# The second block's head outputs are turned in another order, and the branch products begin with the differential branch

## The reference, cut to what matters

```python
o_mla = mla_attention(q, k, v_mla).reshape(b, s, BRANCH_WIDTH)                        # latent heads
od = diff_attention(dq, dk, dv, positions, lam, slopes[WIN_HEADS:])
o_diff = (rms_norm(od, g_diff_out) * (1.0 - lam_init)).reshape(b, s, BRANCH_WIDTH)    # differential heads
o_win = window_attention(wq, wk, wv, positions, win_sink, slopes[:WIN_HEADS])         # banded heads
gates = jax.nn.sigmoid(gate_logits.reshape(b, s, N_BRANCH, D_MODEL))
merged = (gates[:, :, 0] * (o_mla @ w_branch[0])
          + gates[:, :, 1] * (o_diff @ w_branch[1])
          + gates[:, :, 2] * (o_win @ w_branch[2]))
x = x + merged @ w_out
```

## Time and profile before

| | |
|---|---|
| median of three runs | 1748.23 us (1746.33 to 1748.44) |
| the profiled execution, its own time | 1745.46 us |
| its span in the trace | 1743.6 us |
| TensorE busy with matmuls | 1670.2 us of the span |
| VectorE, ScalarE, GpSimd busy | 1172.7, 920.7, 443.6 us |
| mean granted TensorE clock, in parts of full speed | 0.987 |

### The profile page before, as it was taken

One profiled execution on the slowest core, in us unless ns is written; L12 is line 12 of the kernel. 1 busy time (PEld: TensorE's weight loads), 2 busy tenths in 40 slices (PEclk: granted clock), 3 DMA queues, 4 the chain that ended last, 5 costly groups with the idle time before them and its releaser, 6 DMA issues.

```text
span 1743.6 us, 30149 instructions
## 1 busy us (share of the span) xinstructions
PE 1670.2 (96%) x11354; PEld 1520.1 (87%) x11354; DVE 1172.7 (67%) x1609; ACT 920.7 (53%) x1576; POOL 443.6 (25%) x184
## 2 busy tenths in 40 slices
PE   8989999999989999999999999999899999999997
PEld 6878799988887899978899989999788999899996
DVE  5687754458786644476784777666758856777667
ACT  5654544446645544465655564444665555554445
POOL 2212222212222222224511122222235211222222
PEclk9989999999999999999999999999999999999999
DMA  8432455556423655546323455665464333566653
GB/s 329 154 122 91 150 201 181 190 160 208 155 77 115 229 181 182 182 144 227 125 97 111 134 190 183 209 196 177 150 214 156 106 101 115 172 205 199 203 179 126
DMA packets 82563, 288.74 MB, mean 166 GB/s; under 512 B 9051, under 2 KB 11908, under 8 KB 81924
## 3 DMA queue, kind: packets, MB, share of 16 engines
q1 hardware_dynamic: 77352, 272.58, 47.7%
q10 hardware_dynamic: 5084, 14.37, 2.4%
HBM read 284.81 MB, written 2.11 MB: 165 GB/s over the span
## 4 chain that ended last, share of the span: by engine, by line
PE 62%; DVE 7%; ACT 2%; issue 2%; DVEq 0%; ACTq 0%
PE bank L716 30%; PE bank L733 25%; DVE w_lo L682 2%; PE bank L1287 2%; PE bank L1268 1%; PE bank L1259 1%; PE bank L761 1%; PE bank L1247 1%; ACT w_hi L678 1%; PE bank L1300 0%; DVE qk L2513 0%; PE bank L906 0%; PE bank L1179 0%; PE bank L914 0%; DVE z L2105 0%
## 5 line engine op out<-in xcount | busy, mean ns | idle before, releaser
L682 POOL TENSOR_TENSOR w_lo<-raw,w_hi 128x1024 fp32r<-128x1024 f32 x146 | 376.6, 2579 | 1225.6 <-ACT w_hi L678 1225.6
L682 DVE TENSOR_TENSOR w_lo<-raw,w_hi 128x1024 fp32r<-128x1024 f32 x364 | 555.9, 1551 | 155.2 <-ACT w_hi L678 153.8
L678 ACT ACTIVATE w_hi<-raw 128x1024 fp32r<-128x1024 f32 x510 | 519.9, 1051 | 107.3 <-PE bank L716 47.4
L716 PE MATMUL bank<-x_t_hi,w_hi 128*128 128x256 f32 x1984 | 326.7, 287 | 5.5 <-ACT gl L1423 3.0
L716 PE MATMUL bank<-x_t_lo,w_hi 128*128 128x256 f32 x1984 | 319.8, 284 | 0.0
L716 PE MATMUL bank<-x_t_hi,w_lo 128*128 128x256 f32 x1984 | 319.5, 283 | 0.0
L716 PEld LDWEIGHTS bank<-x_t_hi,w_hi 128*128 128x128 f32 x1984 | 279.0, 192 | 18.0 <-issue 5.7
L716 PEld LDWEIGHTS bank<-x_t_lo,w_hi 128*128 128x128 f32 x1984 | 274.5, 192 | 0.0
L716 PEld LDWEIGHTS bank<-x_t_hi,w_lo 128*128 128x128 f32 x1984 | 274.3, 192 | 0.0
L733 PE MATMUL bank<-w_hi,x_t_hi 128*128 128x512 f32 (+3 forms) x448 | 134.5, 383 | 9.1 <-issue 5.8
L733 PE MATMUL bank<-w_hi,x_t_lo 128*128 128x512 f32 (+3 forms) x448 | 131.5, 376 | 1.5 <-DVE x_t_lo L1946 1.5
(11 more groups left out here) (391 smaller groups left out, 2134.5 us busy)
## 6 DMA issues: line engine op xcount, KB each, us to landing
raw<-stream SPq DMA_DIRECT2D x511, 512.0 KB, 4.3
rows<-rows ACTq DMA_DIRECT2D x4, 1024.0 KB, 4.7
gain<-rows ACTq DMA_DIRECT2D x8, 512.0 KB, 4.2
hv_p<-hv_dram ACTq DMA_DIRECT2D x14, 256.0 KB
x<-x_in SPq DMA_DIRECT2D x2, 512.0 KB, 4.9
bias_r<-rev_dram SPq DMA_DIRECT2D x1, 1024.0 KB, 7.3
hv_dram<-hv ACTq DMA_DIRECT2D x2, 512.0 KB, 6.9
y_out<-x SPq DMA_DIRECT2D x2, 512.0 KB, 2.7
```

What stands on the lines that cost most here:

```text
L678: self.eng.activation(w_hi[:, i, :], raw[:, i, :], ACT.Copy).then_inc(hi_done.sem, 1)
L682: self.eng.tensor_tensor(w_lo[:, i, :], raw[:, i, :], w_hi[:, i, :].bitcast(F32), ALU.subtract).then_inc((lo_pool if self.part == "pool" e ...
L716: mm = pe.matmul(target, a[:, i, w0 + kt * P:w0 + (kt + 1) * P], b[:, k0 + kt, :], start=kt + k == 0, stop=k == 2 and kt == kts - 1)
```

## The change

TensorE no longer waits for `o3_ready` ahead of the six pieces. It waits for the banded heads' part instead, turns the four differential and banded pieces, then waits for `o3_ready` and turns the two latent ones. ACT and DVE take the pieces in the same new order. Of the branch products the differential one of output tile 0 (`br1`) comes first, then the latent one (`br0`), then the banded one (`br2`) and the others as before. The bank table follows, so that pieces and products get banks in the new order. Amounts of work and numbers of instructions stay as they are.

```diff
+OT_ORDER = (2, 3, 4, 5, 0, 1)
...
-    work(*[f"ot{j}" for j in range(6)], *[f"br{i}" for i in range(24)])
+    work(*[f"ot{j}" for j in OT_ORDER], "br1", "br0", *[f"br{i}" for i in range(2, 24)])
...
-                pe.wait_ge(*c["o3_ready"](at, 1))
-                for j in range(6):
+                pe.wait_ge(*banks.read(at, "owin"))
+                for j in OT_ORDER:
+                    if j == 0:
+                        pe.wait_ge(*c["o3_ready"](at, 1))
                     transposed(at, f"ot{j}", lambda k, t: o3[:, t, (2 * j + k) * P:(2 * j + k + 1) * P])
 
-                for i in range(24):
+                for i in (1, 0, *range(2, 24)):
                     b = i % 3
                     pe.wait_ge(*banks.free(at, f"br{i}"))
                     if i < 3:
-                        pe.wait_ge(*x_hi(at, 8 + 2 * b))
+                        pe.wait_ge(*x_hi(at, 8 + OT_ORDER.index(2 * b)))
...
                     feature_major(at, uid[f"br{i // 2}"], bank[banks.bank(at, f"br{i}")][:, 0:S], o_t_hi, o_t_lo, 4,
-                                  begin=i % 2 == 0, w0=i % 2 * 512, k0=4 * b, split=split if i < 3 else None).then_inc(*banks.fills(at, f"br{i}"))
+                                  begin=i == 1 or i % 2 == 0 and i > 0, w0=i % 2 * 512, k0=4 * b, split=split if i < 3 else None).then_inc(*banks.fills(at, f"br{i}"))
...
-                for j in range(6):
+                for j in OT_ORDER:
                     if j in (2, 3):
                         round_gained(at, f"ot{j}", o_t_hi[:, 2 * j:2 * j + 2, :], lambda k: par2("g_do"))
...
-                for j in range(6):
+                for n, j in enumerate(OT_ORDER):
                     hi, lo = o_t_hi[:, 2 * j:2 * j + 2, :], o_t_lo[:, 2 * j:2 * j + 2, :]
                     if j in (2, 3):
-                        rest_gained(at, f"ot{j}", 7 + j, hi, lo, lambda k: par2("g_do"))
+                        rest_gained(at, f"ot{j}", 7 + n, hi, lo, lambda k: par2("g_do"))
                     else:
-                        rest_of_bank(at, f"ot{j}", 7 + j, hi, lo)
+                        rest_of_bank(at, f"ot{j}", 7 + n, hi, lo)
```

## The result

The changed kernel took 1750.2 us (median of 18 runs, 1747.91 to 1754.26), the kernel before in the same sessions 1746.53 us. The ratio is 1.0024, with a 95% interval of 1.0016 to 1.0031: 4.2 us slower, most likely. By the medians it is 3.7 us. The change touches two short places of an execution of 1750 us.

A forecast was written before the change was run, and what follows sets the result against it. TensorE, busy 1670.2 of 1743.6 us, was taken as the bound, with ScalarE's sigmoids on the chain before the products. Bank 0.9 + clock 2.2 = 3.1 us on the 1748.23 us median gave 1751.3 us, range 1747.5 to 1753.0.

The forecast's parts named there:

- The waiting engine: Before the branch products: ScalarE's table and sigmoids set the first rounding, so turning pieces during TensorE's 1.67 us wait gains nothing.
- The bank of the first product: Bank 7, held by the third piece, comes free later, so the first product starts 0.43 us later per layer, 0.9 in all.
- my sign of 6.3 to 6.4 us: Sign of being right: first product starts 6.3 to 6.4 us behind the last weighing in both layers, in place of 5.93.
- The latent pieces: Turned, rounded and rested last, they cost the latent product nothing, with 0.6 us of room before its last four matmuls.
- The clock: A 3.0 us TensorE idle stretch before the products drops its clock to half in both layers, costing 2.2 us in all.
- I take 1.1 us: Chosen loss per layer from half clock on the products, out of 0.9 to 1.5 us, for a stretch of 3.4 us.
- the forecast: Main case, chance 0.50: first product 0.43 us later per layer and half clock in both layers; 1750.9 to 1751.7 us.
- slower than can be missed: Rival, chance 0.20: half clock lies wholly on the products in both layers, 3.9 us in all, 1752.1 us or more.
- within 0.2%: Outcome that the whole kernel's time stays within 0.2% (about 3.5 us) of before, given 0.68.
- a real gain: Rival, chance 0.04: without sigmoids ahead of the roundings, 1.67 us come off each layer, 3.3 us in all, 1744.9 us.
- no change: Rival, chance 0.03: the first product is not later and TensorE keeps full speed, 1748.2 us.
- a clock that holds: Rival, chance 0.23: TensorE's speed doesn't fall at the products, or falls in one layer alone; 1749.1 to 1750.2 us.

The follow-up runs named there:

- e2: Changed kernel with the wait for the latent heads put back ahead of the first piece, all orders staying changed; ratio 1.0003 to the kernel before.
- e3: Changed kernel with ScalarE's table load and first two sigmoids moved behind the six roundings; ratio 0.9987 to the kernel before.
- e1: Changed kernel with TensorE's idle stretch filled by 24 useless transposes per layer, ahead of turning the last banded piece; ratio 1.0008 to the kernel before.
- e8: Kernel before with only the two banded pieces moved to idle banks 0 and 1, orders and sigmoids as before; ratio 0.9991.
- e5: e3 with, in addition, the two banded pieces moved to idle banks 0 and 1; ratio 0.9985 to the kernel before.
- e7: Changed kernel run again unaltered for a second profile; ratio 1.0019 to the kernel before.
- e9: e5 with, in addition, ScalarE and VectorE taking the pieces in the order differential, latent, banded; 1739.61 us against 1747.62, ratio 0.9957.
- e4: Kernel before with only ScalarE's table load and two sigmoids moved behind the six roundings, old orders kept; ratio 0.9994.
- e10: e5 run once more unaltered, on another chip; ratio 0.9985 to the kernel before.

## Why the prediction was right, and what was off

**The waiting engine.** Right. The chain said that ScalarE's table and sigmoids set the first rounding and that the early pieces are worth nothing. The first rounding stayed at 3.2 us, e2 shows the same start with and without early pieces, and e3 shows that the pieces become worth something as soon as ScalarE is free.

**The bank of the first product.** Right in mechanism and size: 0.43 us per layer expected, 0.39 measured in e1 and in the second layer of e2. That the bank decides is shown by e8, and by e5 against e3. In the changed kernel itself a second thing stands behind it. At the half clock TensorE's own last eight transposes take 1.94 us, and the first product, which comes behind them in the queue, starts at 6.64 us in place of 6.34 (6.51 in one layer of e7). My sum had the product wait for VectorE alone, so my sign of 6.3 to 6.4 us came in one of the four layers.

**The latent pieces.** Costed at nothing, by 0.6 us of room. Right for the changed kernel: its products have no wait. The room was the reason that it stayed hidden. In e5, where the products start at 2.70 us, the same rests cost 0.58 us, and e9 takes that away.

**The clock.** The mechanism was right, the size too small. The step that failed is "I take 1.1 us". I had let the half clock begin once work comes again, for 3.4 us, with part of it lost on the transposes. In the first profile it began 1.3 us before work came, lasted 6.8 us and cost 2.0 us per layer; in the second it lasted 3.4 us and cost 1.2 and 1.5. The mean of the four is 1.7 us. With it the sum is 2 x (0.39 + 1.7) = 4.2 us, the measured ratio of 1.0024. That the two agree so closely is partly luck, since the first profile is of one of the six long executions among 18. With the second profile alone the sum is 3.5 us, beside 3.3 us by the ratio of e7. The row 115.40 of the earlier trace rows showed a stretch of 6.8 us, and I used it only in the rival. I had also looked only at pauses of 2.5 to 3.3 us. The half clock of the earlier trace rows, from which I took the price, stood behind pauses of 1.2, 0.6 and 1.48 us, so the trace of before already had a fall without a long pause.

**The cases.** The predicted time of 1751.3 us stands beside 1750.2 measured, and the difference to before is 3.7 us by the medians (4.2 by the ratio) where 3.1 was forecast. That the time itself came within 1.1 us is luck: my base of 1748.23 us, the median of three runs, was 1.7 us above the median of 18, and the cost was 0.6 us too small, the other way. The case that came is between the forecast and the rival "slower than can be missed", whose price was 3.9 us. I had given more to "within 0.2%" (0.68) than to "slower" (0.29), and the ratio came out just beyond that bound. The rivals of a real gain and of no change are out by the ratio, and nothing speaks for a clock that holds: all four layers in two profiles of the changed kernel show the fall.

## What to carry to other kernels

Before an engine is given its work earlier, follow the chain from the result backwards: here TensorE's named wait of 1.7 us was covered by ScalarE's table load and sigmoids, and the order of work on ScalarE was the thing to change first. A pause of TensorE can cost more than its length. With two pauses and work between them the clock stayed at 2.4 GHz in both layers of before, and one pause of 3.30 us in their place was followed by the half clock in four layers of four. Splitting a pause is no guarantee, as one layer of e2 shows. Moving useful work, or even useless transposes, into a pause that can't be avoided is worth a try. And where pieces and products share a rotation of buffers, ask which piece lies in the buffer that the first product gets: late sigmoids, two idle banks and another order of the rests, all on top of the change, brought 0.43% over the kernel before.

## What the runs showed of the hardware that was not expected

Two pauses of 1.71 and 1.31 us, with 1.94 us of transposes between them, were followed by the half clock in one layer and not in the other (e2). With one pause of 1.67 us ahead of the transposes it happened once as well (e4). The three pauses of 1.2, 0.6 and 1.48 us were followed by it in the first layer of before and not in the second. So a pause that left the clock alone in one profile is no proof that it will in the next. On this the Trainium skill, "TensorE: Matmul & The Clock Gate", Part 1, says of a kernel's start that the same kernel can meet the change of clock at different matmuls from run to run. The two profiles of the changed kernel show the like in mid-kernel: the first layer's fall came 1.3 us before the transposes in one and 0.3 us behind their start in the other. The half clock came in stretches of 3.4 and of 6.8 us for the same kernel and the same pause of 3.30 us (the changed kernel and e7). The time ahead of the first place, where no edit is, differs between the profiles by 6 us (959.3 us in e10, 965.4 in e9). Single executions therefore can't be compared at this size, but the place can.
